# Moving 30 chunk transposes from TensorE to 32x32 block turns on VectorE and cross-quadrant copies on ScalarE

## The reference, cut to what matters

```python
x = x + swiglu(rms_norm(x, ffn_norm[i]), ...)      # (silu(h @ w_gate) * (h @ w_up)) @ w_down
y = sigmoid(o) * rmsnorm(ht, g_head) * silu(z)     # mixer, per head of 512 columns; then y @ w_out
k, v = ...; q = ...                                # second layer, 16 heads of 128
s = (q_h @ k_h.T) * Dh ** -0.5 + bias              # per head: q and k both stand transposed
y = (softmax(s) @ v_h) * silu(z)                   # then y @ w_out
```

## Time and profile before

| | |
|---|---|
| Device time, 3 runs | 2426.9 us median (2425.92 to 2427.5) |
| Profiled execution | span 2424.4 us from first to last instruction; the median of the runs lies 2.5 us above it |
| Busy | PE 2408.2 us (99%), DVE 1726.8 (71%), ACT 1170.0 (48%), POOL 45.2 (2%) |
| Granted TensorE clock, mean | 0.999 |
| HBM | 574.01 MB read, 238 GB/s over the span |

### The profile page before, as it was taken

How to read it: one execution, slowest core, us unless ns; L and a number is a source line. 1 busy time by engine, 2 the same in 40 slices (tenths; PEclk the granted TensorE clock), 3 DMA queues, 4 the chain that set the end, 5 groups by cost and what they waited for, 6 DMA issues and landing times.

```text
span 2424.4 us, 31019 instructions
## 1 busy us (share of the span) xinstructions
PE 2408.2 (99%) x11417; PEld 1960.0 (81%) x11417; DVE 1726.8 (71%) x2422; ACT 1170.0 (48%) x1583; POOL 45.2 (2%) x65
## 2 busy tenths in 40 slices
PE   9999999999999999999999999999999999999998
PEld 7778888888888888778888888888888778888887
DVE  8885777777777776667778667677676676667665
ACT  6665444444444444554444434444444564455553
POOL 1100000000000000000000000000000000000000
PEclk9999999999999999999999999999999999999999
DMA  8445888888888887567777787767777467776654
GB/s 299 141 136 175 265 292 294 307 294 293 284 296 292 291 297 228 163 225 237 241 232 234 239 265 244 237 231 235 240 232 240 156 193 255 242 238 212 232 192 139
DMA packets 161829, 578.16 MB, mean 238 GB/s; under 512 B 18288, under 2 KB 20592, under 8 KB 161680
## 3 DMA queue, kind: packets, MB, share of 16 engines
q1 hardware_dynamic: 160432, 572.64, 71.3%
q0 software_dynamic: 1104, 3.28, 0.4%
q10 hardware_dynamic: 144, 0.26, 0.0%
HBM read 574.01 MB, written 2.10 MB: 238 GB/s over the span
## 4 chain that ended last, share of the span: by engine, by line
PE 96%; DVE 2%; ACT 1%; DMA 1%; issue 0%; POOL 0%; SPq 0%; DVEq 0%; ACTq 0%
PE PS L1177 30%; PE PS L1179 30%; PE PS L1178 30%; PE PS L796 1%; DVE WL L2165 1%; PE PS L908 1%; DMA X<-in_x 0%; ACT WH L1552 0%; PE PS L803 0%; PE PS L876 0%; DVE X L2132 0%; PE PS L1004 0%; PE PS L1078 0%; PE PS L1024 0%; PE PS L1021 0%
## 5 line engine op out<-in xcount | busy, mean ns | idle before, releaser
L2165 DVE TENSOR_TENSOR WL<-W,WH 128x1024 fp32r<-128x1024 f32 x814 | 991.2, 1224 | 528.6 <-ACT WH L1552 526.0
L1552 ACT ACTIVATE WH<-W 128x1024 fp32r<-128x1024 f32 x814 | 857.4, 1060 | 923.0 <-PE PS L1179 912.6
L1177 PE MATMUL PS<-WH,XTH 128*128 128x512 f32 x2144 | 855.3, 399 | 3.6 <-DVE XTL L1683 1.2
L1179 PE MATMUL PS<-WH,XTL 128*128 128x512 f32 x2144 | 835.9, 390 | 0.0
L1178 PE MATMUL PS<-WL,XTH 128*128 128x512 f32 x2144 | 835.0, 389 | 0.0
L1177 PEld LDWEIGHTS PS<-WH,XTH 128*128 128x128 f32 x2144 | 402.6, 188 | 94.5 <-issue 10.1
L1179 PEld LDWEIGHTS PS<-WH,XTL 128*128 128x128 f32 x2144 | 402.3, 188 | 85.7
L1178 PEld LDWEIGHTS PS<-WL,XTH 128*128 128x128 f32 x2144 | 402.9, 188 | 83.6 <-issue 3.8
L1177 PE MATMUL PS<-WH,YTH 128*128 128x512 f32 x1120 | 441.0, 394 | 2.5 <-DVE WL L2165 1.8
L1179 PE MATMUL PS<-WH,YTL 128*128 128x512 f32 x1120 | 436.2, 389 | 0.0
L1178 PE MATMUL PS<-WL,YTH 128*128 128x512 f32 x1120 | 436.1, 389 | 0.0
(11 more groups left out here) (282 smaller groups left out, 1171.3 us busy)
## 6 DMA issues: line engine op xcount, KB each, us to landing
W<-in_vec SPq DMA_DIRECT2D x192, 512.0 KB, 4.6
W<-in_avoz SPq DMA_DIRECT2D x192, 512.0 KB, 4.5
W<-in_wg SPq DMA_DIRECT2D x88, 512.0 KB, 4.7
W<-in_wu SPq DMA_DIRECT2D x88, 512.0 KB, 4.9
W<-in_wd SPq DMA_DIRECT2D x88, 512.0 KB, 4.7
W<-in_gate SPq DMA_DIRECT2D x64, 512.0 KB, 4.4
W<-in_aqk SPq DMA_DIRECT2D x64, 512.0 KB, 4.4
W<-in_aout SPq DMA_DIRECT2D x64, 512.0 KB, 4.3
```

The source lines that it names most:

```text
L1177: e.matmul(p, x, WH[:, g % NH, j], start=first, stop=False)
L1179: i = e.matmul(p, y, WH[:, g % NH, j], start=False, stop=last)
L1552: e.activation(WH[:, n % NH], W[:, i % NW], ACT.Copy).then_inc(s_hi, 1)
L2165: e.tensor_tensor(l, src, h.bitcast(F32), ALU.subtract).then_inc(s_lo, 1)
```

## The change

PE no longer transposes 30 of the 31 chunks; the last (`ZG` of `band(3)`) stays. In their place:

- DVE turns the 32x32 blocks of each row tile in place of their quadrant: `blocks_T`, two `transpose` of 128x512 into a new buffer `TQ`, one at each of two ticks.
- ACT moves the blocks across quadrants: `quadrants`, 16 copies of 32 partitions x 256 elements (4 x 4 quadrant pairs) from `TQ` into `MT` (a new buffer), `KT` or `Q4`. They are spread 2 to a tick (over 8 ticks), for the queries and `ZG` 4 to a tick.
- From `MT`, ACT writes `YTH` (`pairs_T`) and DVE `YTL` (`pair_lows`), now from SBUF.
- `s_kq` counts chunks, no longer halves. The scratch space of software DMAs is set to 8192 bytes.

ACT and then DVE, the new functions:

```diff
+            def quadrants(number, dst, n, sem):
+                w.wait_ge(s_tq, number)
+                for x in range(16):
+                    a, b = slice(32 * (x // 4), 32 * (x // 4) + 32), x % 4
+                    o = dst[32 * b:32 * b + 32].rearrange("p j (t r) -> p t j r", t=2)[:, :, :, a]
+                    i = e.activation(o, TQ[a].rearrange("p t (j b r) -> p t j b r", j=4, b=4)[:, :, :, b], ACT.Copy)
+                    if x == 15:
+                        i.then_inc(sem, 1)
+                    if x % n == n - 1:
+                        yield
```

```diff
+            def blocks_T(src):
+                for t in range(2):
+                    i = e.transpose(TQ[:, t], src[:, t])
+                    if t:
+                        i.then_inc(s_tq, 1)
+                    yield
```

PE, in `band`:

```diff
             def band(j, free, par, _):
-                yield from to_T("qT", 4 + j)
+                yield from ticks(6)
...
-                    w.wait_ge(s_kq, 8 + 2 * j + 2)
+                    w.wait_ge(s_kq, 4 + j + 1)
...
+                if j < N_BY_DVE:
+                    return
```

ACT, in `ffn` and `band`:

```diff
             def ffn(f, slot, ver, ends, free):
-                yield from ticks(21)
-                for half in range(2):
-                    w.wait_ge(s_unit, free)
-                    halves_T(("mid", f, half), 4 * slot, None)
-                    yield
+                yield from ticks(19)
+                yield from quadrants(TQ_FFN + f + 1, MT, 2, s_mt)
+                w.wait_ge(s_unit, free)
+                yield from pairs_T(MT_FFN + f + 1, 4 * slot, None)
...
             def band(j, free, par, g):
                 qc(4 + j, par, g)
-                yield from to_T("qT", 4 + j, Q4)
+                yield from ticks(2)
+                if j:
+                    w.wait_ge(*filled(("bs", 4 * j - 1)))
+                yield from quadrants(TQ_QS + 2 * j + 1, Q4, 4, s_kq)
...
+                if j < N_BY_DVE:
+                    yield from ticks(2)
+                    yield from quadrants(TQ_BAND + 2 * j + 1, MT, 4, s_mt)
+                    w.wait_ge(s_unit, free)
+                    yield from pairs_T(MT_BAND + j + 1, 4 * j, None)
+                    return
```

DVE, in `band`:

```diff
             def band(j, free, par, g):
                 qc(4 + j, par, g)
-                yield from ticks(6)
+                yield
+                w.wait_ge(s_qc0, 4 + j + 1)
+                w.wait_ge(s_qc1, 4 + j + 1)
+                if j:
+                    w.wait_ge(s_mt, MT_BAND + j)
+                yield from blocks_T(QC)
+                yield from ticks(3)
...
+                if j < N_BY_DVE:
+                    yield
+                    w.wait_ge(s_bo, 4 * j + 4)
+                    w.wait_ge(s_kq, 4 + j + 1)
+                    yield from blocks_T(ZG)
+                    yield from ticks(6)
+                    yield from pair_lows(4 * j, None)
+                    return
```

More of the change, by code:

```diff
@@ L1032, in mix @@
                 gfree[ends[3][0]] = [(s_mix, at("z0")), (s_mix, at("z1"))]
[L1033 to L1050, removed]
+                yield
             def keys(j, par, _):
                 gfree[par] = [(s_qc0, j + 1), (s_qc1, j + 1)]
-                yield from to_T("kT", j)
+                yield
             def values(j, par, _):
@@ L1227, in halves_T, with pairs_T @@
                 i.then_inc(s_yh, 1)
+            def quadrants(number, dst, n, sem):
[8 more added lines that the diff above has]
+                        yield
+            def pairs_T(number, k0, scale):
+                w.wait_ge(s_mt, number)
+                for x in (0, 2):
+                    if scale is None:
+                        i = e.activation(YTH[:, k0 + x:k0 + x + 2], MT[:, x:x + 2], ACT.Copy)
+                    else:
+                        for j in (x, x + 1):
+                            i = e.activation(YTH[:, k0 + j], MT[:, j], ACT.Copy, scale=scale(k0 + j))
+                    i.then_inc(s_yh, 1)
+                    yield
             def turn_x(n, k, g):
@@ L1435, in mix @@
                 e.activation(SG[:, 512:1024], Gb[ends[3][0]][1][:, :], ACT.Sigmoid).then_inc(s_mixa, 1)
[L1436 to L1455, removed]
+                yield from ticks(5)
+                yield from quadrants(TQ_MIX + h + 1, MT, 2, s_mt)
+                base = CGH + 4 * h - 4 * (h % 4)
+                w.wait_ge(s_unit, free)
+                yield from pairs_T(MT_MIX + h + 1, 4 * (h % 4), lambda kt: cols[:, base + kt:base + kt + 1])
             def qc(n, par, g):
@@ L1465, in keys @@
                 qc(j, par, g)
-                yield from to_T("kT", j, KT[:, 4 * j:4 * j + 4])
+                yield from ticks(3)
+                w.wait_ge(s_post, 8)
+                yield from quadrants(TQ_KEYS + j + 1, KT[:, 4 * j:4 * j + 4], 2, s_kq)
             def values(j, par, g):
@@ L1629, in lows_Y, with pair_lows @@
                 i.then_inc(s_yt, 1)
+            def blocks_T(src):
[3 more added lines that the diff above has]
+                        i.then_inc(s_tq, 1)
+                    yield
+            def pair_lows(k0, scale):
+                for x in (0, 2):
+                    n_y[0] += 1
+                    w.wait_ge(s_yh, n_y[0])
+                    if scale is None:
+                        s = slice(k0 + x, k0 + x + 2)
+                        i = e.tensor_tensor(YTL[:, s], MT[:, x:x + 2], YTH[:, s].bitcast(F32), ALU.subtract)
+                    else:
+                        for j in (x, x + 1):
+                            i = e.scalar_tensor_tensor(out=YTL[:, k0 + j], in0=MT[:, j], scalar=scale(k0 + j),
+                                                       in1=YTH[:, k0 + j].bitcast(F32), op0=ALU.mult,
+                                                       op1=ALU.subtract)
+                    i.then_inc(s_yt, 1)
+                    yield
             def mean(sums, n_sq):
@@ L1888, in ffn @@
                     if f:
-                        w.wait_ge(*filled(("mid", f - 1, 0)))
-                        w.wait_ge(*filled(("mid", f - 1, 1)))
+                        w.wait_ge(s_mt, MT_FFN + f)
                     e.scalar_tensor_tensor(out=MID[:, t], in0=Gb[par][t][:, :], scalar=rst[:, t:t + 1],
                                            in1=SGT[:, t], op0=ALU.mult, op1=ALU.mult).then_inc(s_mid, 1)
[L1893 to L1896, removed]
+                yield
+                w.wait_ge(s_mid, 2 * f + 2)
+                yield from blocks_T(MID)
+                yield from ticks(9)
+                yield from pair_lows(4 * slot, None)
             def gate_w(g):
@@ L2017, in mix @@
                     yield
[L2018 to L2022, removed]
+                w.wait_ge(s_mix, at("y1"))
+                w.wait_ge(s_mt, MT_MIX + h)
+                yield from blocks_T(G1)
+                yield from ticks(9)
+                base = CGH + 4 * h - 4 * (h % 4)
+                yield from pair_lows(4 * (h % 4), lambda kt: cols[:, base + kt:base + kt + 1])
             def qc(n, par, g):
```

24 lines of the change are left out of this document (14 added, 10 removed).

## The result

The changed kernel takes 2464.95 us (median of 4 runs, 2461.29 to 2465.82), the kernel before, run beside it, 2426.6 us: ratio 1.0154, 95% interval [1.0139, 1.0168]. It is 38.4 us slower; 12.7 were predicted, and the range ended at 2452.

What follows compares the result with a forecast made beforehand. PE was taken to bound the kernel, busy 99% of the span. Transposes removed -25.5, waits for the queries +33.7 and slow clock +4.5 gave +12.7 us, so 2439.6 us, range 2427 to 2452.

Steps and rivals of the forecast that it cites:

- What bounds the kernel, and what is removed: PE bounds the kernel; each removed group of 16 transposes costs it 0.85 us, 30 groups 25.5 us.
- The duration of a copy: One ACT copy in `quadrants`, 256 elements a partition: 420 ns, from the slope of two rows.
- its step: Start spacing of ACT's copies in a row: 0.32 us each, so 16 copies take 5.1 us.
- the upper end of 0.40: Highest copy step considered, from the 495 ns copy with a scale from SBUF; it would add 9.0 us.
- 112 copies and 13 turns: Copies and DVE turns on the path to `s_kq` over the four bands, used to size the sensitivity of the waits.
- dear copies: Rival, chance 0.13: copies between quadrants with 32-element runs cost 0.50 us or more, 20 us on top, 2460 us.
- Hand-over of the queries: PE waits on `s_kq` before each band's first scores: 10.4 us at three bands, 2.5 at `band(0)`, 33.7 together.
- Clock: PE's clock falls during the three long waits before scores, costing 1.5 us each, 4.5 us in all.
- I cost these at nothing: Feed-forward, mixer and keys, 23 chunks: moved work arrives in time, so PE gets no new wait, 0 us.
- a regular mixer head: Worst covered place: WH ends near 1194.5 instead of 1193.1, but a margin of over 4 us holds.
- The WH tile of 2144.93: ACT's WH tile at `band(0)`, with 23 removed groups before it, stands 19.5 us earlier in the changed profile.
- the high end of copy and clock together: Upper end of the forecast range, 2452 us: copy step 0.40 us (+9.0) with clock loss +4.5.

Runs made afterwards that it cites:

- experiment 1: Only the 23 chunks of feed-forward, mixer and keys moved to DVE and ACT; queries and gated outputs on PE as in the kernel before: 2416.54 us.
- experiment 5: Only the 23 chunks of feed-forward, mixer and keys moved, with both feed-forward turns in one tick and the copies one tick earlier than in the change: 2411.47 us.
- experiment 6: Like experiment 5, but the one feed-forward chunk that meets a late DMA has its copies one slot later: 2408.96 us.
- experiment 9: Full change with 4 copies of 128 partitions for 16 of 32, same strides, no move across quadrants; output not the reference's: 2414.52 us.
- experiment 10: Full change with the 16 copies each written into the quadrant it reads from, same strides; output not the reference's: 2453.49 us.
- experiment 11: Full change with copies across quadrants of 256 contiguous elements in place of 8 runs of 32; output not the reference's: 2461.54 us.
- experiment 12: Full change with the copies reordered: four in a row write one quadrant and read all four in turn: 2463.41 us.
- experiment 2: Only 4 chunks of queries and 3 gated outputs moved to DVE and ACT; all others on PE as in the kernel before: 2475.08 us.
- experiment 7: Full change, but the queries transposed by PE as before; gated outputs still moved, with 16 copies at the start of bands 1 to 3: 2432.49 us.
- experiment 8: Full change, but all 4 gated outputs transposed by PE as before; the 4 chunks of queries stay moved: 2444.18 us.
- experiment 3: Full change with extra matmuls on constants in PE's stream before its wait for the queries (48, at band 0 18): 2458.57 us.

## Why the prediction was wrong in size and right in kind

**What bounds the kernel, and what is removed: right.** 0.88 us a group against 0.85, in the full change and in experiments 1, 5 and 6.

**The duration of a copy: right; its step: wrong.** This is the term of the sum that was mis-sized most. "The next instruction starts about 0.1 us before the end ... so a step is 0.32 us" was read from WH and the queries, which both cover all 128 partitions. The copy lasts 415 ns (420 forecast), but two copies in a row change the quadrant, and these do not overlap: 0.427 us a step. The note "no row shows 32" named the gap, and the upper end of 0.40 was still under it, because both ends took off the same 0.1 us. The term of 112 copies and 13 turns on the path was right: 112 x 0.107 = 12.0 us more, and the waits measured 45.7 against 33.7. This step accounts for the whole difference in the waits. The "dear copies" rival had the right sign, with a threshold of 0.45 us and a cause (a longer copy) that no run bears out. That the overlap is what is lost is shown by experiments 9 to 12.

The Trainium skill ("ScalarE: Activation LUTs", What ACT_TABLE_LOAD costs) lets successive activations overlap by about 93 ns; the rows within a quadrant agree (0.41 less 0.31), those across quadrants do not. For VectorE its "VectorE: DVE Perf Modes" (Two Vector instructions with no wait between them) holds an instruction back until the earlier ones have ended, where the first quadrant that it reads or writes is another than before; experiments 10 and 12 show this pattern on ScalarE.

**Hand-over of the queries: right.** Place, semaphore, number (four, three long) and the order of ACT and DVE came out as walked. Experiments 1 and 2 show that the bands carry all the net loss, 7 and 8 that queries and gated outputs each bring a part.

**Clock: too small by half.** 1.5 us each for three waits were read from the kernel's first 13 matmuls. Behind a wait in mid-kernel it was 1.7 to 3.0 us, and band 0, whose wait of 4.4 us I had left out, paid 1.7 as well: 9.1 against 4.5. Experiment 3 shows that the time is the clock's. The clock dipped at the late row too (2.4 of the 6.0 us), where the prediction has no dip.

**"I cost these at nothing": wrong by 9.7 us.** The reasoning for a regular mixer head holds: no head waits. It was taken over unchecked to the feed-forward and keys. The three exceptions are where another task's rare instructions meet the copies: the late row (6.0 us, experiments 5 and 6), the last feed-forward group, where only 8 slots lie between chunk and use (1.3 us, gone in experiment 5), and the keys, with two waits of 0.55 us for WL (2.4 us in all; 0.3 in experiment 9, so they too hang on the time of the copies). The WH tile of 2144.93 should have come 19.5 us earlier. It came at 2134.95 us, 10.0 earlier: 20.2 saved, less 9.7 and less 0.6 at the kernel's start.

**The difference in all.** Between +12.7 and the +38.9 us of the profile stand 12.0 us for the copies' step, 4.6 for the clock, 9.7 for what was put at nothing and 0.8 not assigned, less 0.9 because a removed group had cost 0.88 us and not 0.85. Nearly all of it pushes the same way, so the direction does not rest on errors that cancel. The upper end of the range, named as the high end of copy and clock together, is by these terms 2453.1, not 2452.

**The skill's rule for TensorE** ("VectorE: DVE Perf Modes", Rules for kernel authors: a 128x128 transpose goes to TensorE where PSUM will do) holds for the chunks with a short deadline, where the change lost 48.9 us. For 23 of the 30 it does not decide: experiment 6 has them on VectorE and ScalarE, and is 17.4 us faster.

## What to carry to other kernels

Work taken off the bounding engine pays only where the engines that take it over have slack before the point of use: sort the places by deadline, and move only those with slots in between (here 23 of 30, placed as in experiment 6: -17 us instead of +38). Price a run of small copies by their start spacing in their own sequence of partitions, not by their duration less an overlap read elsewhere. And look at every place once where a moved instruction stands beside a wait that is harmless today.

## What the runs showed of the hardware that was not expected

- ScalarE copies of 32 partitions x 256 elements start 0.31 us apart while they stay in one quadrant, 0.41 to 0.43 us apart where the quadrant read or written changes (experiments 9 to 12). Copies of 128 partitions also start 0.31 us apart, and strides of 32-element runs change nothing.
- VectorE's turn of 128x512 floats in 32x32 blocks takes 701 ns, 0.6 us a step: the price of a copy of that size out of PSUM (684 ns).
- Idle times of TensorE of 3.6 us (near 440 us) and 4.25 us (band 0) were enough in the full change to lose the upper clock level; the work behind took 2.4 and 1.7 us longer.
- The same length of wait does not always have the same effect. Behind 1.9 us the clock fell in experiments 3 (the row of 0.75) and 9 (7.83 us from the first score to the second; 6.25 and 6.22 behind the other two), but not behind the WL wait of 1.93 us at `band(1)` of the full change (1.00 from 2198 to 2204 us). Behind 3.03 us near 440 us in experiment 11 it stayed at 1.00 as well.
